# Router product with the weight held, embedding products inside the retention, and the first expert's halves loaded in pairs

## The reference, cut to what matters

```
y_b = _retention(q_b, k_b, v)             # 8 heads, 4 chunks of 128 rows, a state from chunk to chunk
y_b = _group_norm(y_b, gain, bias) * silu(r_g)
x   = x + concatenate([y_a, y_b]) @ w_out
hn  = _rmsnorm(x, g_ffn_norm)             # x * rsqrt(mean(x*x) + eps) * g
logits = hn @ w_router + b_router         # 1024 x 32: 32 experts
top 4 experts of each row, softmax over the four = gates
x   = x + sum over the 4 of gate * expert(hn)       # blocks of 128 rows of one expert
x   = x + (p @ w_ple_proj) * sigmoid(_rmsnorm(x, g_ple) @ w_ple_gate)   # p: 512 x 256
```

## Time and profile before

| | us |
|---|---|
| median of 3 runs | 2404.69 (2403.54 to 2411.37) |
| the profiled execution | 2396.49 |
| its span in the trace | 2394.6 |
| retention, first scores to first output projection | 995.2 to 1034.2 |
| output projection | 1034.2 to 1079.3 |
| norm, embedding products, transposes | 1079.3 to 1105.5 |
| router product | 1105.5 to 1116.2 |
| routing until the first expert product | 1116.2 to 1134.7 |
| one step of the expert loop, later on | 35.4 |

### The profile page before, as it was taken

One profiled execution on the slowest core, in us unless ns is written; L12 is line 12 of the kernel. 1 busy time (PEld: TensorE's weight loads), 2 busy tenths in 40 slices (PEclk: granted clock), 3 DMA queues, 4 the chain that ended last, 5 costly groups with the idle time before them and its releaser, 6 DMA issues.

```text
span 2394.6 us, 30384 instructions
## 1 busy us (share of the span) xinstructions
PE 2250.1 (94%) x10452; PEld 1820.1 (76%) x10452; DVE 1810.6 (76%) x1895; ACT 1382.9 (58%) x1535; POOL 261.9 (11%) x173
## 2 busy tenths in 40 slices
PE   5998897999998998886999999999999999999998
PEld 3866676888787886674778888888888888888866
DVE  7887635555634585856889999999999999999975
ACT  4355524333413244414577787787777777778763
POOL 1000000000000000001041221221121122122110
PEclk8999798999999998987999999999999999999999
DMA  9530312233122320226899999999999999999970
GB/s 334 183 120 1 123 36 93 83 106 106 40 83 71 120 71 1 97 67 239 338 354 387 386 379 395 382 382 391 384 382 385 387 386 375 398 384 378 394 260 36
DMA packets 184930, 569.88 MB, mean 238 GB/s; under 512 B 10492, under 2 KB 34975, under 8 KB 184831
## 3 DMA queue, kind: packets, MB, share of 16 engines
q1 hardware_dynamic: 172239, 523.69, 57.2%
q0 software_dynamic: 12624, 45.28, 6.9%
HBM read 542.71 MB, written 26.23 MB: 238 GB/s over the span
## 4 chain that ended last, share of the span: by engine, by line
PE 85%; DVE 7%; ACT 3%; issue 2%; DMA 1%; SPq 1%; POOL 0%; DVEq 0%; ACTq 0%; POOLq 0%
PE bank L1826 11%; PE bank L1828 11%; PE bank L1832 11%; PE bank L1470 7%; PE bank L1471 7%; PE bank L1472 7%; PE bank L1451 4%; PE bank L1821 4%; PE bank L1820 4%; PE bank L1819 4%; PE bank L1668 3%; PE bank L1669 3%; PE bank L1670 3%; PE bank L1548 2%; PE bank L1530 1%
## 5 line engine op out<-in xcount | busy, mean ns | idle before, releaser
L2576 DVE TENSOR_TENSOR w_lo<-stage,w_hi 128x2048 fp32r<-128x2048 f32 x396 | 886.0, 2286 | 61.6 <-ACT w_hi L1304 53.4
L1304 ACT ACTIVATE w_hi<-stage 128x2048 fp32r<-128x2048 f32 x396 | 740.6, 1921 | 78.7 <-PE bank L1832 53.4
L1826 PE MATMUL bank<-w_hi,xeT_hi 128*128 128x512 f32 x792 | 262.5, 413 | 0.0
L1828 PE MATMUL bank<-w_hi,xeT_lo 128*128 128x512 f32 x792 | 246.2, 392 | 0.0
L1832 PE MATMUL bank<-w_lo,xeT_hi 128*128 128x512 f32 x792 | 212.8, 391 | 0.0
L2022 DVE TENSOR_TENSOR ring_low<-ring,half_top 128x2048 fp32r<-128x2048 f32 (+2 forms) x42 | 93.1, 2221 | 150.5 <-ACT half_top L1026 150.1
L1472 PE MATMUL bank<-half_top,hT_low 128*128 128x512 f32 (+1 forms) x480 | 187.6, 391 | 0.0
L1828 PEld LDWEIGHTS bank<-w_hi,xeT_lo 128*128 128x128 f32 x792 | 149.8, 189 | 32.6
L1826 PEld LDWEIGHTS bank<-w_hi,xeT_hi 128*128 128x128 f32 x792 | 147.9, 190 | 34.0 <-issue 0.6
L1832 PEld LDWEIGHTS bank<-w_lo,xeT_hi 128*128 128x128 f32 x792 | 149.6, 189 | 31.3
L1026 ACT ACTIVATE half_top<-ring 128x2048 fp32r<-128x2048 f32 (+2 forms) x42 | 77.8, 1856 | 164.6 <-PE bank L1472 160.1
(11 more groups left out here) (477 smaller groups left out, 4260.8 us busy)
## 6 DMA issues: line engine op xcount, KB each, us to landing
stage<-in_w_up_gate SPq DMA_DIRECT2D x264, 1024.0 KB, 8.3
stage<-in_w_down SPq DMA_DIRECT2D x132, 1024.0 KB, 7.0
ring<-in_w_ada SPq DMA_DIRECT2D x12, 2048.0 KB, 9.2
ring<-in_w_up SPq DMA_DIRECT2D x22, 1024.0 KB, 7.7
ring<-in_w_in SPq DMA_DIRECT2D x10, 2048.0 KB, 7.9
ring<-in_w_out SPq DMA_DIRECT2D x4, 2048.0 KB, 12.9
ring<-in_w_down SPq DMA_DIRECT2D x4, 2048.0 KB, 8.4
stage<-in_w_ple_gate SPq DMA_DIRECT2D x4, 1024.0 KB, 9.1
```

The lines of the kernel that those rows point to most:

```text
L1304: fn(w_hi[top_of(h)][:, :], src[:, :], ACT.Copy).then_inc(s_hi, 1)
L1826: mm(bank[b][:, :], hi[:, k0 + k, :], wh[:, k, at_[b]:at_[b] + CW], start=first and k == 0, stop=False)
L1828: mm(bank[b][:, :], lo[:, k0 + k, :], wh[:, k, at_[b]:at_[b] + CW], start=False, stop=False)
L2576: tt(w_lo[h][:, :], stage[h][:, :], w_hi[top_of(h)][:, :].bitcast(FP), ALU.subtract).then_inc(s_lo, 1)
```

## The change

In the order of the program:

- The input rows `ptok` and the projection weights of the embedding are loaded ahead of the retention. PE turns the rows (`pT`) ahead of the first scores, and makes the embedding products of tile n inside retention step n, behind `out_T(3, n - 1)` and ahead of `ret_scores(n + 2)`. ACT copies them to two small buffers, and POOL writes them out. Buffers and `ptok` lie in ring slot 0, so SP loads `wout2` half 1 only when all four tiles have been written.
- The projection's half 0 uses banks 0 to 3 and half 1 banks 4 to 7. The transposes for the router are made of `x` itself, before the norm, those of tile t-1 behind the products of tile t.
- The router: its weight is multiplied by the gain once, and is the stationary operand; the rows stream. Each tile's result goes to 32 partitions of its own (`b[t * NE:(t + 1) * NE, 0:P]`). DVE copies it, PE turns it back, DVE multiplies by the reciprocal root and adds the bias.
- The normalised rows for the gather are scaled on ACT (`scaled3`) and multiplied by the gain on DVE (`gained3`), each tile in a buffer of its own.
- Halves 0 and 1 of the first expert are loaded once the embedding products are made, 2 and 3 after the projection's half 0, 4 to 7 after half 1. ACT and DVE split 0 to 2 inside the projection.
- In the routing, the sums of the gates move behind the row numbers of the first block, and their transposes on PE into the first slot.
- POOL gathers one slot further ahead: the rows of slot 2 before the loop, those of slot i+2 in step i.

```diff
-    ptok = at(R + 48 * KB, [P, NT, 256], name="ptok")
-    pT = at(R + 52 * KB, [P, 2, S], name="pT")
+    ptok = at(0, [P, NT, 256], name="ptok")
+    pT = at(4 * KB, [P, 2, S], name="pT")
+    pp_out = [at((8 + 4 * i) * KB, [P, D], name=f"pp_out{i}") for i in range(2)]
+    junk3 = at(R + 32 * KB, [P, D], name="junk3")
+    xn3 = [at(R + o * KB, [P, D], name=f"xn3_{i}") for i, o in enumerate((70, 74, 60, 64))]
...
+        for m in range(2):
+            product(("ple", n, m), (5 + m) if n % 2 else m)
...
+            full(sp, ("win2", 6, NT - 1))
+            sp.dma_start(ptok[:, :, :], v["p_2"][0, 0].rearrange("(t p) n -> p t n", p=P)).then_inc(s_ptok, 16)
+            load(number[("ple",)])
             full(sp, ("S", 2, 4 * H - 1))
             sp.dma_start(gnrow[:, 0, :], row_bcast(v["ret_gn_gain_2"][0, :], CW)).then_inc(s_gn, 16)
             sp.dma_start(gnrow[:, 1, :], row_bcast(v["ret_gn_bias_2"][0, :], CW)).then_inc(s_gn, 16)
-            for i in range(number[("wout2", 0)], ND):
-                load(i)
+            load(number[("wout2", 0)])
+            for parity in range(2):
+                sp.wait_ge(s_pp[parity], 16 * NT // 2)
+            load(number[("wout2", 1)])

             full(sp, ("oT", 3, NT - 1))
             sp.dma_start(grow_f[:, :], row_bcast(v["g_ffn_norm_2"][0, :], D)).then_inc(s_grf, 16)
             sp.dma_start(wrt[:, :, :], w["w_router_2"].rearrange("(k p) n -> p k n", p=P)).then_inc(s_wrt, 16)
             sp.dma_start(brt[:, :], row_bcast(v["b_router_2"][0, :], NE)).then_inc(s_wrt, 16)
-            sp.dma_start(ptok[:, :, :], v["p_2"][0, 0].rearrange("(t p) n -> p t n", p=P)).then_inc(s_ptok, 16)
             sp.dma_start(conc[:, :], v["consts"][:, packs["c"][0]:packs["c"][0] + packs["c"][1]]).then_inc(s_conc, 16)
             sp.dma_start(bsum[:, :], v["b_up_gate_2"][0]).then_inc(s_bsum, 16)
...
+                if h == 0:
+                    full(sp, ("ple", NT - 1, 1))
+                elif h == 2:
+                    full(sp, ("wout2", 0, NT - 1))
+                elif h == 4:
+                    full(sp, ("wout2", 1, NT - 1))
                 expert(h, 0, False)
...
+            for t in range(NT):
+                for n in range(2):
+                    taken(pool, ("ple", t, n))
+                pool.dma_start(pp_d[t * P:(t + 1) * P, :], pp_out[t % 2][:, :]).then_inc(s_pp[t % 2], 16)
...
             gather()
+            pool.wait_ge(s_got, 32)
+            index(idx_in, 2, 2)
+            rows_turned(2)
+            gather()
             pool.wait_ge(s_slots, 1)
             nb = n_slots(pool)
             with pool.Fori(1, nb) as i:
-                pool.wait_ge(s_got, 16 * i + 16)
-                index(idx_in, i + 1, 2 * i)
-                rows_turned(2 * i)
+                pool.wait_ge(s_got, 16 * i + 32)
+                index(idx_in, i + 2, 2 * i + 1)
+                rows_turned(2 * i + 2)
                 pool.nop().then_inc(s_held, 1)
                 gather()
                 pool.wait_ge(s_scat, 16 * i)
-                index(idx_out, i - 1, 2 * i + 1)
+                index(idx_out, i - 1, 2 * i + 2)
                 output_stands(i - 1)
                 scatter()
...
                 ret_root(n)
+                embedding(n)
                 if n in (1, 2):
                     top(("wout2", 0), n - 1)
             out_T(3, NT - 1)
             top(("wout2", 1), 0, 1)
...
+            def square3(t):
+
+                act_e.wait_ge(s_xr, 3 * NT + t + 1)
+                k = 3 * NT + t
+                link(fn(junk3[:, :], x[:, t, :], ACT.Square, accum_out=stat[:, k:k + 1]))
+                fn(stat[:, 20 + k:21 + k], stat[:, k:k + 1], ACT.Sqrt, scale=1.0 / D, bias=eps[:, 0:1]).then_inc(s_sq, 1)
+            def scaled3(t):
+
+                k = 40 + 3 * NT + t
+                act_e.wait_ge(s_rms3, t + 1)
+                if t == 2:
+                    act_e.wait_ge(s_zd, 16)
+                    act_e.wait_ge(s_scat, 16)
+                fn(xn3[t][:, :], x[:, t, :], ACT.Copy, scale=stat[:, k:k + 1]).then_inc(s_xr3, 1)
...
-            split_hi(0, 0, 1, 2, 3)
+            act_e.wait_ge(s_b3, 1)
+            split_hi(0, 0, 1, 2)
+            square3(0)
+            square3(1)
+            columns3(0)
+            square3(2)
+            columns3(1)
+            square3(3)
+            columns3(2)
+            scaled3(0)
+            columns3(3)
+            for t in range(1, NT):
+                scaled3(t)
+            full(act_e, ("wout2", 1, NT - 1))
+            split_hi(0, 3)
...
                 if n:
                     out_T(3, n - 1, o2)
+                embedding(n)
                 if n < 2:
                     ret_scores(n + 2)
...
+                project(("wout2", n), lambda t: ("wout2", n, t), lambda k, t: out_top[k // 4][:, k % 4, t * P:(t + 1) * P], of(hT_low),
+                        then=(lambda t: columns3(t - 1) if t else None) if n else None)
+            columns3(NT - 1)
+            pe.wait_ge(s_wg, 1)
             b = acquire(("router",))
             for t in range(NT):
                 hT_stands(3, t)
-                for k in range(KT):
-                    ins = mm(b[:, t * NE:(t + 1) * NE], hT[:, k, t * P:(t + 1) * P], wrt[:, k, :], start=k == 0, stop=k == KT - 1)
+            for k in range(KT):
+                for t in range(NT):
+                    ins = mm(b[t * NE:(t + 1) * NE, 0:P], wrt[:, k, :], hT[:, k, t * P:(t + 1) * P], start=k == 0, stop=k == KT - 1)
             publish(ins, ("router",))
+            pe.wait_ge(s_lT, 1)
+            publish(tr(acquire(("logits",))[:, 0:P], logitsT[:, :]), ("logits",))
...
+            tt(wrt[:, :, :], wrt[:, :, :], bc(vec[:, VGF:VGF + KT], 2, [P, KT, NE]), ALU.mult).then_inc(s_wg, 1)
+            split_lo(0, 0, 1, 2)
...
+            residual2(1, 0)
+            residual2(1, 1)
+            root3(0)
+            columns3(0)
+            residual2(1, 2)
+            root3(1)
+            columns3(1)
+            residual2(1, 3)
+            root3(2)
+            columns3(2)
+            gained3(0)
+            columns3(3)
+            root3(3)
+            gained3(1)
+            label = ("router",)
+            b = full(dve, label)
+            take(ve.tensor_copy(logitsT[:, :], b[:, 0:P]), label)
+            taken(dve, label)
+            dve.nop().then_inc(s_lT, 1)
+            gained3(2)
+            b = full(dve, ("logits",))
+            dve.wait_ge(s_rms3, NT)
+            take(tt(logits[:, :, :], b[:, 0:P].rearrange("p (t e) -> p t e", t=NT), bc(stat[:, 52:56], 2, [P, NT, NE]), ALU.mult), ("logits",))
+            taken(dve, ("logits",))
+            link(tt(logits[:, :, :], logits[:, :, :], bc(brt[:, :], 1, [P, NT, NE]), ALU.add))
...
             tt(gate4[:, :, :], top8[:, :, 0:4], top8[:, :, 0:1].broadcast_to([P, NT, 4]), ALU.subtract).then_inc(s_top8, 1)
+            gained3(3)
...
+            dve.wait_ge(s_ge, 1)
+            link(ve.reduce_sum(den[:, 0:4], gate4[:, :, :], axis=AX))
+            link(ve.reciprocal(den[:, 0:4], den[:, 0:4]))
+            link(tt(gate4[:, :, :], gate4[:, :, :], bc(den[:, 0:4], 2, [P, NT, 4]), ALU.mult))
+            link(tt(gate_eq[:, :, :, :], eq4[:, :, :, :], gate4[:, :, :].unsqueeze(3).broadcast_to(wide), ALU.mult))
```

215 lines of the change are left out of this document (107 added, 108 removed).

## The result

The changed kernel took 2384.72 us in the median of four runs (2383.88 to 2389.12), the kernel before 2404.88 beside it: ratio 0.9925, 95% interval 0.9905 to 0.9945. It is faster by 0.75%, and 4.3 us faster than the 2389.0 of the forecast.

The account below looks back on a forecast made before the run. PE was taken as the bound (94% busy, loop step 35.40 us), savings ahead of the loop counting one for one; 10.9 - 20.1 - 3.8 + 2.8 + 0.5 - 6.0 = -15.7 gave 2380.8, median 2389.0; range 2376 to 2399.

Parts of the forecast that it names:

- 1, retention: Embedding products inside the retention, partly covered by PE's waits for DVE: +4.0 us in all, bounds +1 to +10.
- The 1.7 us of clock in half 0: Output projection, half 0: first products at full clock as PE idles less before, 21.7 instead of 23.4 us, -1.7.
- 2, the bias wait: Between the projection's halves: `bsum` queued behind half 1's weights, PE stands 5.2 us, slow clock after +1.7; bounds none to 10.
- twice as long: Sign of a wrong forecast: PE's wait of some 5 us between the halves is missing or twice as long.
- bias in time: Rival: `bsum` lands by 1045, say because short loads don't queue behind the weights; gives back 5.2 + 1.7, 2382; chance 0.14.
- 3, half 1: Projection's half 1: three groups of eight transposes at 0.9 us, two ahead of the last product, +1.7; slow clock +1.7.
- 4, projection to router: From the projection's end to the router: a chain of 6.1 us in place of 26.2, -20.1.
- 5, router: Router's 64 records at the scores' 0.107 each: 6.8 us, -3.8; bounds 1.7 (four tiles at once) and 13.7 (half clock).
- tiles side by side: Rival: the router's four column tiles run at once on PE, 5.1 us better in sum, 2383.9; chance 0.18.
- the half clock of another rival: Rival: router products one after another at half clock after PE's pause, +6.8 us, 2395.8; chance 0.10.
- 6, routing: From the router to the first expert product: added copies, turn and sums, gates' sums moved; +2.8 us in sum.
- 7, gather: Loop's second step: gathering one slot ahead removes a 4.1 us wait and 1.9 slow start, -6.0; between 0 and -6.

Follow-up runs that it names:

- e1_small_first: Changed kernel with the five short loads, `bsum` among them, issued ahead of the wait for embedding rows and half 1's weights: 2375.74 us, ratio 0.9878.
- e5_gained_early: Changed kernel with the gain products of row tiles 2 and 3 ahead of DVE's copy of the router's result: 2382.96 us, ratio 0.9924.

## Why the prediction was right, and where it was not

*What bounds it.* Right: what was saved ahead of the loop stood at the end (ten lines of the ledger add up to -15.1, and the last is the one that the change does not explain), and the loop's step stayed 35.4 us.

*1, retention.* The groups cost 3.2 us for a forecast of 4.0; leaving out half of each gave 2.8 back, so the price is PE's products and not ACT's copies. The 1.7 us of clock in half 0 came true in the first trace alone (22.0 us), in the second half 0 took 23.6; it is worth nothing either way, as shown above. Counting it as a gain was wrong in its logic: a faster stretch ahead of a wait for something else only lengthens the wait.

*2, the bias wait.* The mechanism is as forecast and is shown twice over (moving the loads, or moving the low half, takes it away). The size was off: 10.0 us, 8.5 in the second execution, for 5.2, close to the forecast's own sign of being wrong ("twice as long"). Two sub-terms were wrong in opposite directions. SP was to send the weights at 1036 and `bsum` at 1038.8; they went out at 1037.35 and 1046.14, because the short issues behind a 2 MB load took up to 4.68 us each, in the kernel before all six took 0.34 to 0.58 us. And `bsum` was to land 11.7 us behind its issue; it took 6.9. So DVE started at 1053.09, 2.6 us later than forecast, while PE was ready 2.2 us earlier, 1.8 of it by the earlier start. The rival "bias in time" rested on short loads not queueing behind the weights; they do, at the issue.

*3, half 1.* +4.2 for +3.4: the two groups of transposes cost 1.7 us as said (`e1_small_first`, without a pause, took 46.98 us for both halves, 23.6 + 21.7 + 1.7), the slow clock after the pause 2.5 in place of 1.7 (mean granted clock of the stretch 0.91).

*4, projection to router.* -20.2 for -20.1; the chain is the one written down, with DVE waiting 2.22 us for ACT's first scaled rows.

*5, router.* The step that failed: 6.8 was taken, 3.62 measured. The row that I extrapolated from, the scores, is one of products that follow one another; the rival of tiles side by side, which had 0.18, is what happened, and with it the half clock of another rival, which had 0.10. I had written that no row showed two products of PE at once and so gave the lower bound (1.7) too little weight. Run one after another the router takes 8.8 us: my 0.107 a record holds there at full clock (0.109), but 3.4 us of it ran at half, so that my 6.8 would have been wrong the other way. The two rivals pull against one another: a quarter of 6.8, twice, is 3.4.

*6, routing.* +2.8 for +2.8, but by two chains that end together, of which I saw one. DVE's reduction to `slot_f` ends at 1122.87 with the gates' sums ahead of it, as forecast. The other is new: the first gather went out 3.5 us behind its index (before about 1), since the last normalised rows had not landed (the weights held back, it was 1.0), and ACT split the turned rows at 1122.31 and 1123.16. Each alone would have given the same time, and this is why an index 1.5 us earlier (`e5_gained_early`) gave 0 to 0.4. That the rows' writes would meet the first expert's weights, half of which are sent just then, was in none of my steps.

*7, gather.* -5.9 for -6.0, and +6.5 when undone. Against the second trace of the kernel before it is -4.1 (70.75 for 74.88): the wait of 4 us is in all three traces that have the old order, the slow start behind it, 1.9 in the forecast, in two of them.

The forecast's first expert product, 1124.5, was met by 1124.59: 4.8 us too little for the pause and 0.8 for half 1 were cancelled by 3.2 too much for the router, 0.8 for the retention and the start that came 1.8 earlier. That they cancel is luck. The sum for the spans was 4 us too good against the first pair of traces (-15.7 for -11.7), of which 3.4 are the line at the loop's end, at the clock shown there. Against the second pair it is 2 us too good. The medians, 19 to 20 us apart, are further than either pair of traces. The 2389.0 rests on one more term: I added the 8.2 us by which the kernel before's median lay above its profiled execution. The changed kernel's profiled execution lies on its median (2384.75 and 2384.72), so that this term was 8.2 too much; the sum's 4.0 in the other direction leave the 4.3 by which the forecast missed, within its range. The two traces that lie within 2 us of their kernels' medians are the second of before and the first of the changed kernel; their spans are 18.8 us apart, and 4.8 of these are the start (997.59 and 992.83). Two starts of the kernel before don't tell whether its start is usually later, so this part stays open.

## What to carry to other kernels

When a load is put behind a wait in a queue, price the loads queued behind it by their issue too: a short load that the next engine needs belongs ahead of a long one, even if it is needed later. A forecast should say, at each join of two chains, how late the second one is; where two end together, a gain on one is nothing, and a second cure for the same wait can undo the first. When output has 32 columns, let consecutive products go to different 32-partition places, and not only different outputs.
